# A two-layer hybrid decoder on one core: the post-norm factors go through DRAM to all partitions

## What is computed

```python
mods = jnp.einsum('bd,lde->lbe', jax.nn.silu(c), ada_w) + ada_b[:, None, :]
for i in range(DEPTH):
    sh_m, sc_m, g_m, sh_f, sc_f, g_f = jnp.split(mods[i][:, None, :].astype(x.dtype), 6, axis=-1)
    h = rms_norm(x, norm_w[i, 0]) * (1 + sc_m) + sh_m
    y = ab_mixer(h, ...) if i % 2 == 0 else cd_mixer(h, ...)
    x = x + g_m * rms_norm(y, norm_w[i, 1])
    h = rms_norm(x, norm_w[i, 2]) * (1 + sc_f) + sh_f
    y = conv_ffn(h, ...)
    x = x + g_f * rms_norm(y, norm_w[i, 3])
return x
```

## Time and profile before

| | us |
|---|---|
| median of 3 runs | 1022.4 |
| lowest and highest run | 1020.86 and 1023.63 |
| span of the profiled execution, first to last instruction | 1018.2 |
| own time of the profiled execution | not given apart from the runs; 4.2 more than its span if it is the median |
| TensorE busy | 974.2 (96%) |
| VectorE busy | 776.2 (76%) |
| ScalarE busy | 616.1 (61%) |
| DMA traffic | 195.29 MB, 192 GB/s over the span |

### The profile page before, as it was taken

How to read it: one execution, slowest core, us unless ns; L and a number is a source line. 1 busy time by engine, 2 the same in 40 slices (tenths; PEclk the granted TensorE clock), 3 DMA queues, 4 the chain that set the end, 5 groups by cost and what they waited for, 6 DMA issues and landing times.

```text
span 1018.2 us, 24681 instructions
## 1 busy us (share of the span) xinstructions
PE 974.2 (96%) x8661; PEld 899.0 (88%) x8661; DVE 776.2 (76%) x1650; ACT 616.1 (61%) x1396; POOL 18.3 (2%) x18
## 2 busy tenths in 40 slices
PE   5999989989999999999999989999999999999997
PEld 3999977867899999888999989889887899999786
DVE  1688546677778888988788888876679988888855
ACT  2666656675766666447666676664464576666444
POOL 0000000000000000000000000113000000000000
PEclk9999999999999999999999999999999999999999
DMA  9867673637665666883577644233117746666562
GB/s 349 303 174 241 237 310 125 240 125 256 238 209 176 181 182 184 290 318 116 167 246 227 200 164 155 63 105 91 58 44 265 276 162 184 185 182 178 176 193 97
DMA packets 55829, 195.29 MB, mean 192 GB/s; under 512 B 6179, under 2 KB 8355, under 8 KB 55628
## 3 DMA queue, kind: packets, MB, share of 16 engines
q1 hardware_dynamic: 55756, 194.30, 58.0%
HBM read 193.20 MB, written 1.07 MB: 191 GB/s over the span
## 4 chain that ended last, share of the span: by engine, by line
PE 80%; DVE 9%; ACT 3%; DMA 3%; SPq 2%; issue 2%; DVEq 0%; ACTq 0%
PE proj L579 55%; PE acc L579 24%; DVE w_lo L1764 2%; DMA bias_scratch<-bias_vec 1%; SPq L496 1%; ACT w_hi L1298 1%; DMA ada_first<-in_ada_stream 1%; DMA raw<-in_w_stream 1%; SPq L469 1%; PE acc L849 1%; DVE conv L1840 1%; DVE ada_sum L1779 1%; DVE yn L1935 0%; DVE y_mix L2165 0%; DVE x L1942 0%
## 5 line engine op out<-in xcount | busy, mean ns | idle before, releaser
L1764 DVE TENSOR_TENSOR w_lo<-raw,w_hi 128x512 fp32r<-128x512 f32 x522 | 354.3, 685 | 75.6 <-ACT w_hi L1298 74.1
L1298 ACT ACTIVATE w_hi<-raw 128x512 fp32r<-128x512 f32 x522 | 323.2, 624 | 128.2 <-PE acc L579 103.0
L579 PE MATMUL proj<-h_hi,w_hi 128*128 128x256 f32 x1384 | 396.7, 287 | 4.1 <-DVE conv L1840 1.4
L579 PE MATMUL proj<-h_hi,w_lo 128*128 128x256 f32 x1384 | 393.4, 284 | 0.0
L579 PE MATMUL proj<-h_lo,w_hi 128*128 128x256 f32 x1384 | 393.3, 284 | 0.0
L579 PEld LDWEIGHTS proj<-h_hi,w_hi 128*128 128x128 f32 x1384 | 267.4, 193 | 7.8 <-issue 2.2
L579 PEld LDWEIGHTS proj<-h_lo,w_hi 128*128 128x128 f32 x1384 | 267.6, 193 | 0.0
L579 PEld LDWEIGHTS proj<-h_hi,w_lo 128*128 128x128 f32 x1384 | 267.6, 193 | 0.0
L579 PE MATMUL acc<-w_hi,a_hi 128*128 128x512 f32 x304 | 121.7, 400 | 2.2 <-DVE w_lo L1764 1.2
L579 PE MATMUL acc<-w_lo,a_hi 128*128 128x512 f32 x304 | 118.6, 390 | 0.0
L579 PE MATMUL acc<-w_hi,a_lo 128*128 128x512 f32 x304 | 118.5, 390 | 0.0
(11 more groups left out here) (333 smaller groups left out, 1199.9 us busy)
## 6 DMA issues: line engine op xcount, KB each, us to landing
raw<-in_w_stream SPq DMA_DIRECT2D x264, 512.0 KB, 3.6
ada_long<-in_ada_stream SPq DMA_DIRECT2D x40, 512.0 KB, 7.2
ada_first<-in_ada_stream SPq DMA_DIRECT2D x24, 512.0 KB, 5.1
ada_out<-in_ada_stream SPq DMA_DIRECT2D x12, 512.0 KB, 5.0
ada_mid<-in_ada_stream SPq DMA_DIRECT2D x8, 512.0 KB, 6.9
ada_ssd<-in_ada_stream SPq DMA_DIRECT2D x8, 512.0 KB, 4.9
ada_ssd<-in_ada_stream SPq DMA_DIRECT2D x8, 256.0 KB, 12.0
bias<-bias_scratch SPq DMA_DIRECT2D x2, 1024.0 KB, 5.9
```

The lines of the kernel that those rows point to most:

```text
L579: return pe.matmul(out, a, b, start=start, stop=stop, skip_group_check=True)
L1298: act.activation(hi, src, ACT.Copy).then_inc(w_rounded, 1)
L1764: dve.tensor_tensor(lo, src, hi.bitcast(F32), ALU.subtract).then_inc(w_split, 1)
```

## The change

The eight products, the two copies and their two semaphores are gone. In their place SyncE stores the 128 x 8 factors to a DRAM scratch of 4 x 1024 numbers so that they lie in order of channel (`store_gain`), and later loads that row of 4 KB into each of the 128 partitions (`load_gain`, 512 KB written to SBUF). Both stand in SyncE's list: the store after unit 11 of out0, unit 3 of down0, unit 3 of q1 and unit 9 of down1; the load after unit 13 of out0, unit 7 of down0, unit 14 of out1 and unit 13 of down1. VectorE waits for `gain_landed` where it waited for `g_copied`. ScalarE keeps the small square root.

```diff
+        GAIN_AT = (3, 5, 7, 9)
+            def store_gain(post):
+
+                sp.wait_ge(gain_made, GAIN_AT[post])
+                dst = bass.AP(tensor=gain_scratch.tensor, offset=post * D_MODEL, ap=[[1, P], [P, DT]])
+                sp.dma_start(dst, gain[:, post // 2, 2 * (post % 2) + 1], allow_slow_non_contiguous=True).then_inc(gain_stored, 16)
+
+            def load_gain(post):
+
+                sp.wait_ge(gain_stored, 16 * post + 16)
+                sp.dma_start(G_ROWS[post].rearrange("p a c -> p (a c)"),
+                             gain_scratch[post:post + 1, :].broadcast_to([P, D_MODEL])).then_inc(gain_landed, 16)
...
-            stream(n_out0 + 7, n_up0 + 4)
+            stream(n_out0 + 7, n_out0 + 12)
+            store_gain(0)
+            stream(n_out0 + 12, n_out0 + 14)
+            sp.wait_ge(d_mmat, 12)
+            load_gain(0)
+            stream(n_out0 + 14, n_up0 + 4)
...
             stream(n_up0 + 4, n_down0 + 4)
+            store_gain(1)
             for k in range(12):
+                if k == 4:
+                    sp.wait_ge(y_scaled, 4)
+                    load_gain(1)
                 load_w(n_down0 + 4 + k)
...
             stream(n_q1 - 4, n_q1 + 4)
+            store_gain(2)
             stream(n_q1 + 4, n_q1 + 7)
...
+            load_gain(2)
             stream(n_out1 + 15, n_up1 + 4)
...
-            stream(n_up1 + 4, UNITS)
+            stream(n_up1 + 4, n_down1 + 10)
+            store_gain(3)
+            stream(n_down1 + 10, n_down1 + 14)
+            load_gain(3)
+            stream(n_down1 + 14, UNITS)
...
-                    if k == (10 if cnt == MIX_T else 16):
-                        spread_gain(post)
-
-            def spread_gain(post):
-
-                layer, which = post // 2, 2 * (post % 2) + 1
-                pe.wait_ge(gain_made, 4 * layer + which + 2)
-                for k in range(DT):
-                    last = mm(G_BANKS[post][k // 4][:, (k % 4) * P:(k % 4) * P + P], bc(gain[:, layer, which, k:k + 1], P, P), C("ident"))
-                last.then_inc(g_spread, 1)
...
-                pe.wait_ge(g_copied, 2 * post + 2)
...
-            pe.wait_ge(g_copied, 2)
...
-                            gain_rows(POSTS.index(name))
+                            act.activation(M("root_table", 0, 1), EPS, ACT.Sqrt)
...
-                act.wait_ge(g_spread, post + 1)
-                for a in range(2):
-                    act.activation(G_ROWS[post][:, a], G_BANKS[post][a][:, :], ACT.Copy).then_inc(g_copied, 1)
-                act.activation(M("root_table", 0, 1), EPS, ACT.Sqrt)
...
-                dve.wait_ge(g_copied, 2 * post + 2)
+                dve.wait_ge(gain_landed, 16 * post + 16)
```

More of the change, by code:

```diff
@@ L125, in bucket_rows, with build @@
     return r
-def build(nc, w_dram, ada_dram, x_dram, prm_dram, row_dram, cst_dram, bucket_dram, rel_dram, scratch, out_dram):
+def build(nc, w_dram, ada_dram, x_dram, prm_dram, row_dram, cst_dram, bucket_dram, rel_dram, scratch, gain_scratch, out_dram):
     with ExitStack() as ctx:
@@ L284, in build @@
         vec_mm, vec_copied = sem("vec_mm"), sem("vec_copied")
-        gain_made, g_spread, g_copied = (sem(n) for n in ("gain_made", "g_spread", "g_copied"))
+        gain_made, gain_stored, gain_landed = (sem(n) for n in ("gain_made", "gain_stored", "gain_landed"))
         y_first, y_sqd, y_part, y_root, y_scaled, x_ready = (
@@ L568, in _ @@
                 load_ada(m)
-            stream(n_up1 + 4, UNITS)
+            n_down1 = PARTS["down1"][0]
+            stream(n_up1 + 4, n_down1 + 10)
[3 more added lines that the diff above has]
+            stream(n_down1 + 14, UNITS)
             for q, (b, c) in enumerate(((0, slice(0, D_MODEL)), (1, slice(0, 512)), (1, slice(512, D_MODEL)))):
@@ L781, in spread_rows, with keep_busy @@
                 return last
-            def keep_busy(post, name, count):
+            def keep_busy(name, count):
                 n = PARTS[name][0]
-                pe.wait_ge(g_copied, 2 * post + 2)
                 s, at, _ = freed[before[n]]
@@ L1226, in _ @@
             accumulate(1, range(FT))
-            keep_busy(1, "dt1", 4)
+            keep_busy("dt1", 4)
             turn_x(2, 0, range(4))
@@ L1262, in _ @@
             accumulate(2, range(4, MIX_T))
-            keep_busy(2, "up1", 4)
+            keep_busy("up1", 4)
             turn_x(3, 0, range(4))
@@ L1377, in copy_unit @@
                 return lambda k, i, j, ps: act.activation(dst(k), ps, fn).then_inc(copied, 1)
-            def gain_rows(post):
-                act.wait_ge(g_spread, post + 1)
-                for a in range(2):
-                    act.activation(G_ROWS[post][:, a], G_BANKS[post][a][:, :], ACT.Copy).then_inc(g_copied, 1)
-                act.activation(M("root_table", 0, 1), EPS, ACT.Sqrt)
             def post_norm(post):
@@ L2571 @@
     scratch = nc.dram_tensor("bias_scratch", (AH, 2, 384), F32).ap()
+    gain_scratch = nc.dram_tensor("gain_scratch", (4, D_MODEL), F32).ap()
     out = nc.dram_tensor("out_tiles", (P, NB, D_MODEL), F32, kind="ExternalOutput").ap()
-    build(nc, *aps, scratch, out)
+    build(nc, *aps, scratch, gain_scratch, out)
     r = run_bass_kernel_spmd(nc, [{f"in_{k}": a for k, a in arrays.items()}], core_ids=[0])
```

1 line of the change is left out of this document (removed).

## The result

| us | before | after |
|---|---|---|
| median (12 runs each) | 1021.78 | 1026.34 |
| lowest and highest run | 1020.63 and 1023.93 | 1023.44 and 1030.16 |
| profiled execution, span | 1018.2 | 1025.6 |
| TensorE busy | 974.2 | 972.2 |
| share of the chain of waits on TensorE, VectorE, DMA | 80%, 9%, 3% | 69%, 14%, 9% |

The ratio is 1.0041, with a 95% interval of 1.003 to 1.0052: slower, by more than the 0.3% that a measurement can tell. The forecast of 1016.9 and its whole range are missed. The rival that happened is the slow store, given 9%. The own time of the profiled execution of after is 1027.4, 1.8 above its span, and every run on record lies 1.7 to 1.9 above its own. So of the 4.2 us by which the prediction set the median above the span, some 2.4 are the distance of that one execution from the median.

The account below looks back on a forecast made before the run. TensorE, busy 96% of the span, was taken as the bound, VectorE in out1. Gains of 1.8 + 1.6 + 0.3 + 1.8 = 5.5 us off 1018.2 gave 1012.7, with 4.2 added a median of 1016.9 us, range 1014.3 to 1020.8.

Parts of the forecast that it names:

- the slow store: Rival at all four ends: 4-byte writes take 13 us, weight units wait behind, kernel at 1036.1 us; chance 9%.
- What bounds the kernel, and the gain: TensorE bounds, except VectorE in out1; removal returns 1.8 us after out0, 1.6 down0, 0.3 out1, 1.8 down1.
- The load: Factors' 512 KB broadcast at each end: 3.6 us like a weight unit, counted 0; 1.4 us as down0's other bound.
- the tightest place: Out0, store and load two units apart: unit 14 landing in 4.4 us, factors' traffic 1.4, leaving the store 8.2.
- The price of the store: Each end's store of 1024 4-byte pieces: 4 us to landing, between rows of 2.1 and 6.5; counted 0.
- The upper bound: Store's landing time: at most 6.5 us, from the bias load with as many pieces of 1 KB each.
- The Trainium skill's rule: On the store: a non-contiguous last dimension becomes one descriptor per element and should be rearranged; cited against the change.
- The threshold: Store after out0 may take 8.2 us before anyone suffers, from 241.3 to SyncE's latest issue of unit 14 at 249.5.
- The 10.4 us: Store time from which the change is slower by more than 0.3%: 8.2 + (5.5 + 3.1) / 4, 160 ns per piece.
- The rival's mechanism: SyncE sits in its wait for a slow 4-byte store and weight units stand behind it; chance 9%.
- The rival's price: Store of 13 us loses 13 - 8.2 = 4.8 us at each end, 19.2 for four, giving 1036.1; chance 9%.
- The signs named in advance: Wrong if store lands later than 8 us, ScalarE waits for `raw` at any end, or out1 gives its 1.8 us.

## Why the prediction was wrong

- **What bounds the kernel, and the gain.** Right. The sum was 5.5 us, and without any factor traffic 5.5 us came back by the ratio. Taken by place: out0 1.8 as said, down0 2.0 for 1.6, out1 0.4 for 0.3, down1 1.8 as said. VectorE's rows in out1 moved by only 0.4 us in the change too: in the changed kernel the post-norm there still follows its splits with no wait.
- **The load.** Right in what it costs: counted 0, and with the loads alone the kernel is as fast as without. Its own time was too short: 5.9 to 8.8 us behind the stores, where the sum of the tightest place had 3.6 and 1.4.
- **The price of the store.** This is the step that failed: "I take 4 us, between them, as the pieces are short but as many." It takes 9.9 to 13.3 us. What failed is the reckoning by the pieces' size and number, with nothing for where they lie. The upper bound, 6.5 us from the bias load with as many pieces, was no bound. That row shows 1024 pieces read from DRAM. The store writes them, and the runs show that writes have a price that no row of the profile contained: small pieces that lie side by side, in every slow run those of different partitions. With the addresses 64 bytes apart the same 1024 pieces land in 3.1 to 5.3 us, about the 4 of the forecast, and cost the kernel nothing. For an operation with no row of its own kind, the upper end should have been left open.
- **The Trainium skill's rule.** Its rule on elements, cited in the prediction from "DMA: Bandwidth & Descriptors", pointed in the right direction. The trace bears out the warning, but not its measure: the number of elements is the same in the kernels that lose nothing. The Trainium skill has on the same page, under Specifications, that below 512 bytes a DMA engine reads, modifies and writes. All three forms of 1024 pieces are below that, so this alone doesn't tell the slow one from the others either. The estimate of 0.7 us for 64 packets, from that page, was for the packets alone. The trace has them all recorded between 243 and 245 us, and the landing comes 9 us later.
- **The threshold.** The 8.2 us up to which a store hurts nobody is not contradicted: 6.2 us did no harm, 9.9 did. It was worked out for SyncE's wait, which is not the wait that costs, so part of that is luck. The 10.4 us from which the change would be slower by over 0.3% was not tested; the stores of the change average 11.9.
- **The rival's mechanism was half right.** It had SyncE "in its wait for the store and the weight units stand behind it". SyncE does wait, 9.6 us in two places. But stores that nobody waits for lose 8.1 us. The units that come late are those issued *behind* the store and *ahead of* the wait. I had looked at who waits for the store, and not at what stands behind it on the DMA engines.
- **The rival's price was too high.** It had four equal ends, 13 - 8.2 = 4.8 us each. The store in q1 is the slowest (13.3 us) and costs nothing, since there ScalarE never waits for a weight. The other three lose 3.2, 4.7 and 1.9 us on TensorE. The 4.7 of down0 contain 1.7 us of lower clock after the stall, which was in no case of mine.
- **The signs named in advance.** "I am wrong if the store lands later than 8 us, if ScalarE waits for `raw` at any end": both are in the profile, 12.1 us and 6.5 us. SyncE's wait for the store, expected under 3 us in out0 and 0 elsewhere, is 8.6 there and 1.0 in down0. The roundings of out0 are 1.30 and 1.42 apart, 2.72 for two, up to 249.10, as said, and then stop.

The ends of the post-norm, for comparison with the earlier trace rows. The changed kernel's VectorE at down0, out1 and down1:

```profile
461.26 0.48 DVE L1785 TENSOR_SCALAR ada_sum<-ada_long,c_cols 128x512 f32<-128x512 f32 x1 [2.95 <-DMA ada_long<-in_ada_stream]
...
472.32 0.68 DVE L1944 TENSOR_TENSOR yn<-acc,g_rows 128x512 f32<-128x512 f32 x1
...
816.83 0.68 DVE L1944 TENSOR_TENSOR yn<-acc,g_rows 128x512 f32<-128x512 f32 x1
...
1017.63 0.69 DVE L1944 TENSOR_TENSOR yn<-acc,g_rows 128x512 f32<-128x512 f32 x1 [1.48 <-ACT y_junk L1400]
```

The first post-norm product of down0 comes 5.9 us later than before (466.46), that of out1 7.0 later (809.81), that of down1 7.4 (1010.24). No row waits for the factors, and the 1.66 us wait of down0 is gone, both as the prediction had it; the wait for modulation weights is 2.95 us where it was 2.16. At the last end the 1.48 us wait for ScalarE is the same to the hundredth. TensorE's new wait in out1 is smaller than the 1 us I expected:

```profile
813.94 0.47 PE L607 MATMUL acc<-w_hi,a_hi 128*128 128x512 f32 x1 [0.44 <-DVE w_lo L1773]
```

**What stays open.** The mechanism behind it; how long a stretch must be shared (64 bytes apart is enough, and between 4 and 64 no distance was tried for 1024 pieces of neighbouring partitions); whether it is a shared short stretch or the small range of addresses as a whole (4 KB against 16 and 64); whether partitions count, or the DMA engines that serve them; and how much of the gain from 8- and 32-byte pieces is due to fewer pieces and how much to fewer writers in a line.

## What to carry to other kernels

Before a small vector goes to DRAM element by element, ask which elements lie side by side there and which partitions they come from. If neighbours are single elements from different partitions, turn it first (one TensorE product of 128x8 and one copy here), or keep the pieces apart. Count the cost of a DMA not only by who waits for it but by what is queued behind it, and another issuing queue did not get around it here. And where the trace has no row for an operation, a row of the other direction (read for write) is no upper bound.

## What was not expected of the hardware

- **Neighbouring 4-byte writes of different partitions** hold up the DMA traffic behind them: 9.9 to 13.3 us for 4 KB, with loads behind it landing in 12.6 us where the same two took 3.6 and 4.6. 64 bytes apart, the store lands in 3.1 to 5.3 us and the loads in 5.6.
- **A step of eight elements** in VectorE's second operand (float32, first operand in PSUM) makes 128x512 take 1.10 us instead of 0.68.
- **The clock after a stall.** After a wait of 2.95 us TensorE's products went at 0.43 us for some microseconds (granted clock 0.88 over 14 us), after one of 3.2 us in out0 they did not. In the run without factors the clock fell at another place, with a wait of 1.40 us ahead of it. TensorE's timeline there, the stretch around it, and the same instruction in the kernel before:

```profile
962.27 0.61 PE L596 MATMUL proj<-cst,ada_sum 128*128 128x1 f32 x4 [1.40 <-DVE ada_sum L1777]
```

```profile
955.00:980.00 25.00, 23.60 (x101) 19.09 (x100) 15.62 (x29) 9.40 (x16) 0.00 (x0) 0.93 0.59 176
```

```profile
963.99 0.61 PE L579 MATMUL proj<-cst,ada_sum 128*128 128x1 f32 x4 [1.40 <-DVE ada_sum L1779]
```

The kernel before has the same wait of 1.40 us and a clock of 1.00 in that stretch. So a term of some 1.7 us comes and goes between kernels, and a difference of that size in one profiled execution should not be put down to the edit before the clock has been read.
